# A hybrid decoder layer in split float32: a new order of the first pairs of each FFN, a smaller fold, and the mean added by ScalarE

## The reference

```python
h = rms_norm(x, ffn1_norm[l])
x = x + 0.5 * swiglu(h, ffn1_w1[l], ffn1_w3[l], ffn1_w2[l])   # (silu(h @ w1) * (h @ w3)) @ w2, D_FF = 2816
h = rms_norm(x, mix_norm[l])
proj = h @ w_in[l]                     # q, k, v, z, xBC, dt: attention heads and Mamba-2 heads
...
x = x + concat([attn, ssd]) @ w_out[l]
h = rms_norm(x, ffn2_norm[l])
x = x + 0.5 * swiglu(h, ffn2_w1[l], ffn2_w3[l], ffn2_w2[l])
return rms_norm(x, final_norm)
```

## Time and profile before

| | us |
|---|---|
| median of 3 runs | 582.42 |
| profiled execution, its own time | 582.91 |
| its span | 580.8 |
| TensorE busy | 543.7 (94%) |
| VectorE busy | 438.7 (76%) |
| ScalarE busy | 330.5 (57%) |
| GpSimd busy | 62.2 (11%) |
| bytes moved | 98.15 MB, 169 GB/s in the mean |

### The profile page before, as it was taken

The page is one execution under the profiler, slowest core; times in us unless marked ns, Lnnn a source line. Parts: engine busy times, 40 slices in busy tenths (PEclk is TensorE's granted clock), DMA queues, the critical chain, the costliest instruction groups (busy, mean ns, idle before and its releaser), DMA issues.

```text
span 580.8 us, 9795 instructions
## 1 busy us (share of the span) xinstructions
PE 543.7 (94%) x3676; PEld 500.0 (86%) x3676; DVE 438.7 (76%) x658; ACT 330.5 (57%) x527; POOL 62.2 (11%) x94
## 2 busy tenths in 40 slices
PE   5959999999999989999999999997799999999995
PEld 4948989999999968998888688786699999999993
DVE  3497979888888685768666666558889888888956
ACT  4455556555555466766765874356456555565543
POOL 1000300000000160330532002010000000000014
PEclk9997999999999999999999999999799999999999
DMA  8935776665555438465524225252656665555401
GB/s 249 320 119 181 199 255 217 217 217 172 188 171 186 139 126 247 146 183 157 169 73 146 73 89 179 95 197 62 204 193 217 217 217 178 185 177 183 144 1 72
DMA packets 69434, 98.15 MB, mean 169 GB/s; under 512 B 1812, under 2 KB 55248, under 8 KB 69408
## 3 DMA queue, kind: packets, MB, share of 16 engines
q1 hardware_dynamic: 68560, 95.34, 51.0%
q0 software_dynamic: 848, 2.47, 1.6%
HBM read 96.75 MB, written 1.05 MB: 168 GB/s over the span
## 4 chain that ended last, share of the span: by engine, by line
PE 78%; DVE 8%; DMA 5%; ACT 4%; issue 2%; POOL 1%; SPq 0%; POOLq 0%; DVEq 0%; ACTq 0%
PE bank L1349 24%; PE bank L1350 24%; PE bank L1351 24%; DMA raw<-in_ffn_w 5%; DVE w_lo L915 2%; ACT w_hi L543 2%; PE bank L1481 1%; ACT decay L792 1%; ACT z_silu L571 1%; DVE x_tok L1031 1%; DVE x L929 1%; POOL mean_sq L439 1%; PE bank L1629 1%; PE bank L1630 1%; PE bank L1616 1%
## 5 line engine op out<-in xcount | busy, mean ns | idle before, releaser
L1349 PE MATMUL bank<-hT_hi,w_hi 128*128 128x256 f32 x736 | 210.8, 286 | 13.3 <-DVE tok_rows L1050 13.3
L1350 PE MATMUL bank<-hT_lo,w_hi 128*128 128x256 f32 x736 | 210.1, 285 | 0.0
L1351 PE MATMUL bank<-hT_hi,w_lo 128*128 128x256 f32 x736 | 209.9, 285 | 0.0
L915 DVE TENSOR_TENSOR w_lo<-raw,w_hi 128x1024 fp32r<-128x1024 f32 x132 | 163.5, 1243 | 31.9 <-ACT w_hi L543 31.2
L543 ACT ACTIVATE w_hi<-raw 128x1024 fp32r<-128x1024 f32 x132 | 138.8, 1056 | 61.4 <-PE bank L1351 37.9
L1349 PEld LDWEIGHTS bank<-hT_hi,w_hi 128*128 128x128 f32 x736 | 142.9, 194 | 16.1 <-issue 13.3
L1350 PEld LDWEIGHTS bank<-hT_lo,w_hi 128*128 128x128 f32 x736 | 143.0, 194 | 1.5
L1351 PEld LDWEIGHTS bank<-hT_hi,w_lo 128*128 128x128 f32 x736 | 143.0, 194 | 0.0
L1349 PE MATMUL bank<-w_hi,hT_hi 128*128 128x512 f32 (+1 forms) x192 | 70.1, 365 | 1.4 <-DVE w_lo L915 1.1
L1351 PE MATMUL bank<-w_hi,hT_lo 128*128 128x512 f32 (+1 forms) x192 | 68.2, 355 | 0.0
L1350 PE MATMUL bank<-w_lo,hT_hi 128*128 128x512 f32 (+1 forms) x192 | 68.0, 354 | 0.0
(11 more groups left out here) (198 smaller groups left out, 794.1 us busy)
## 6 DMA issues: line engine op xcount, KB each, us to landing
raw<-in_ffn_w SPq DMA_DIRECT2D x54, 1024.0 KB, 5.4
raw<-in_w_in SPq DMA_DIRECT2D x16, 1024.0 KB, 5.5
tok_rows<-in_ffn_w SPq DMA_DIRECT2D x10, 1024.0 KB, 4.9
raw<-in_w_out SPq DMA_DIRECT2D x6, 1024.0 KB, 4.9
raw<-in_ffn_w SPq DMA_DIRECT2D x4, 512.0 KB, 7.6
x<-in_x SPq DMA_DIRECT2D x4, 256.0 KB, 4.1
out_x<-normed SPq DMA_DIRECT2D x4, 256.0 KB, 2.0
norm_w<-in_ffn_norm SPq DMA_DIRECT2D x1, 512.0 KB, 6.4
```

The lines of the kernel that those rows point to most:

```text
L915: dve.tensor_tensor(lo, src, hi, ALU.subtract).then_inc(half_ready, 1)
L1349: pe.matmul(dst, lhs[0], rhs[0], start=start, stop=False, skip_group_check=True)
L1350: pe.matmul(dst, lhs[0], rhs[1], start=False, stop=False, skip_group_check=True)
L1351: return pe.matmul(dst, lhs[1], rhs[0], start=False, stop=stop, skip_group_check=True)
```

## The change

It has five parts.

1. **First pairs.** `first_pair` of ScalarE and VectorE takes the work on w2 (left half, sums, corner) to its head, and split (1, 1, 0) before the copy of the transposed product. Pair 1 gets a list of its own, `second_pair`, in which the silu stands first.
2. **Slots.** In FFN 1 the odd halves lie in slots 3 and 5 (2 and 3 before) and the rest of w2 in slot 2 (5 before). So mix half 1 no longer waits for the last second products, and mix half 2 does.
3. **Fold.** Two of the four sums are left out; product 5 is added straight to the right quarters of x by VectorE (`fold_right`). GpSimd still adds four times, in the order (0,0), (0,1), (1,1), (1,0); in FFN 1 `row_rstd(1, 0)` stands ahead of the last.
4. **Mean.** GpSimd adds EPS to the left half's sum as soon as that is there; ScalarE adds the right half's sum to it; GpSimd takes the power. This is done in all four norms of 1024 columns.
5. **Rows.** After FFN 1 the second 128 rows are scaled and weighed in one VectorE instruction for each half (`scale_both`), the first 128 not. After FFN 2 the left halves are (`norm_left`). VectorE's and ScalarE's lists after FFN 1 change order: `mix_hi(2)` comes ahead of the squares, the constants and the dt weights go behind. `keep_clock` ahead of z0 writes z0's bank.

```diff
-FFN_SLOT = ((0, 1, 2, 3), (2, 3, 0, 1))
-SPLIT_LEFT, SPLIT_REST = 4, 5
+FFN_SLOT = ((0, 1, 3, 5), (2, 3, 0, 1))
+SPLIT_LEFT, SPLIT_REST = 4, (2, 5)
...
+            def row_rstd(n, t):
+                r = 2 * (n % 2) + t
+                pool.wait_ge(sq_ready, sq_count(n, t) + 1)
+                pool.tensor_scalar(mean_sq[:, r:r + 1], sumsq[:, 0, r:r + 1], EPS, None, ALU.add).then_inc(left_mean_ready, 1)
+                pool.wait_ge(mean_ready, 2 * n + t + 1)
+                pool.tensor_tensor(rstd[:, r:r + 1], row_mean[:, r:r + 1], minus_half[:, :], ALU.pow).then_inc(rstd_ready, 1)
...
-                for j, (t, c, part) in enumerate(((0, 0, T4), (0, 1, T2), (1, 0, T3), (1, 1, T1))):
+                for j, (t, c, part) in enumerate(((0, 0, T4), (0, 1, T1), (1, 1, T3), (1, 0, T3))):
...
+                    if j in (1, 2):
+                        pool.wait_ge(fold_sum, 4 * n + j)
+                    if j == 3 and n == 0:
+                        row_rstd(1, 0)
...
+                if c == 1:
+                    act.wait_ge(sq_ready, sq_count(n, t) + 2)
+                    act.wait_ge(left_mean_ready, 2 * n + t + 1)
+                    act.activation(row_mean[:, r:r + 1], sumsq[:, 1, r:r + 1], ACT.Identity,
+                                   bias=mean_sq[:, r:r + 1]).then_inc(mean_ready, 1)
...
             def first_pair(n):
 
+                left_hi(n, 0, 0)
                 pair_silu(n, 0)
+                sum4_hi(n, 0)
+                corner_hi(n, 0, 0)
                 act.wait_ge(pair_used, n + 1)
                 ffn_hi(n, 1, 0, 0)
+                sums_hi_part(n, 0)
                 pair_silu(n, 1)
                 ffn_hi(n, 1, 0, 1)
-                left_hi(n, 0, 0)
+                ffn_hi(n, 1, 1, 0)
                 act.wait_ge(pair_T, 2 * n + 2)
                 both = bank[:, PAIR_T_BANK, :].rearrange("p (j l) -> p j l", j=2)
                 act.activation(gu_hi[:, :, :], both, ACT.Copy)
                 act.activation(gu, both, ACT.Copy).then_inc(pair_copied, 1)
-                sum4_hi(n, 0)
-                ffn_hi(n, 1, 1, 0)
                 ffn_hi(n, 1, 1, 1)
+
+            def second_pair(n):
+
+                silu(n, 1, 0)
+                asum_hi_part(n, 0)
+                product_hi(n, 1, 0, P)
+                left_hi(n, 1, 1)
+                ffn_hi(n, 2, 0, 0)
+                sum4_hi(n, 1)
+                ffn_hi(n, 2, 0, 1)
+                silu(n, 1, 1)
+                product_hi(n, 1, 1)
+                ffn_hi(n, 2, 1, 0)
+                ffn_hi(n, 2, 1, 1)
...
+            def norm_left(n, t):
+                dve.wait_ge(rstd_ready, rstd_count(n) + t + 1)
+                r, left = 2 * (n % 2) + t, slice(0, 512)
+                dve.scalar_tensor_tensor(normed[:, t, left], x[:, t, left], rstd[:, r:r + 1], norm_w[:, n % 2, left],
+                                         ALU.mult, ALU.mult).then_inc(scaled_left, 1)
...
+            def fold_right(n, t):
+
                 dve.wait_ge(last_products, 3 * n + 2)
-                half_bank(T2, 5, T1).then_inc(fold_sum, 1)
-                dve.wait_ge(last_products, 3 * n + 3)
-                half_bank(T3, 7, T1).then_inc(fold_sum, 1)
-                dve.wait_ge(fold_sum, 4 * n + 3)
-                half_bank(T1, 5, T3).then_inc(fold_sum, 1)
+                dve.wait_ge(folded, 4 * n + t + 2)
+                xs = x[:, t, 512:1024]
+                dve.scalar_tensor_tensor(xs, bank[:, P_BANK[5], :], 0.5, xs, ALU.mult, ALU.add).then_inc(fold_sum, 1)
...
             def first_pair(n):
 
+                pair_sums(n, 0, 0)
+                pair_sum4(n, 0, 0)
                 pair_mul(n, 0)
+                left_lo(n, 0, 0)
+                sum4_lo(n, 0)
+                corner_lo(n, 0, 0)
                 ffn_lo(n, 1, 0, 0)
+                sums_lo_part(n, 0)
                 pair_mul(n, 1)
                 ffn_lo(n, 1, 0, 1)
-                pair_sums(n, 0, 0)
-                pair_sum4(n, 0, 0)
-                left_lo(n, 0, 0)
+                ffn_lo(n, 1, 1, 0)
                 dve.wait_ge(pair_copied, n + 1)
                 dve.tensor_tensor(gu_lo[:, :, :], gu, gu_hi[:, :, :].bitcast(f32), ALU.subtract).then_inc(gu_split, 2)
-                sum4_lo(n, 0)
-                ffn_lo(n, 1, 1, 0)
+                operand_sums(n, 0)
                 ffn_lo(n, 1, 1, 1)
-                operand_sums(n, 0)
+
+            def second_pair(n):
+                up_silu(n, 1, 0)
+                asum_lo_part(n, 0)
+                pair_sums(n, 1, 1)
+                pair_sum4(n, 1, 1)
+                product_lo(n, 1, 0, P)
+                left_lo(n, 1, 1)
+                ffn_lo(n, 2, 0, 0)
+                sum4_lo(n, 1)
+                ffn_lo(n, 2, 0, 1)
+                up_silu(n, 1, 1)
+                operand_sums(n, 1)
+                ffn_lo(n, 2, 1, 0)
+                product_lo(n, 1, 1)
+                ffn_lo(n, 2, 1, 1)
...
+            mix_lo(1)
+            update_x(1, 0, 0)
+            fold_right(0, 0)
+            update_x(1, 0, 1)
+            weigh_x(1, 0, 0)
+            weigh_x(1, 0, 1)
+            scale_left(1, 0)
+            update_x(1, 1, 0)
+            fold_right(0, 1)
+            update_x(1, 1, 1)
+            norm_lo(1, 0)
+            mix_lo(2)
+            scale_both(1, 1)
+            mix_lo(3)
+            norm_lo(1, 1)
...
             ffn_steps(1)
+            fold_right(1, 0)
             update_x(3, 0, 0)
             update_x(3, 0, 1)
-            weigh_x(3, 0, 0)
+            fold_right(1, 1)
+            weigh_x(3, 0, 1)
             update_x(3, 1, 0)
-            weigh_x(3, 0, 1)
             update_x(3, 1, 1)
-            scale_left(3, 0)
-            weigh_x(3, 1, 0)
             weigh_x(3, 1, 1)
-            scale_left(3, 1)
+            norm_left(3, 0)
+            norm_left(3, 1)
```

More of the change, by code:

```diff
@@ L496, in _ @@
             for t in range(TT):
-                rsqrt(2 * t + 2, t, D)
+                row_rstd(0, t)
             pool.wait_ge(first_products, 2)
@@ L503, in _ @@
             pool.dma_start(norm_w[:, 0, :], norms[2].partition_broadcast(P)).then_inc(norm_loaded[2], 16)
-            for t in range(TT):
-                rsqrt(4 + 2 * t + 2, 2 + t, D)
-            pool.wait_ge(weighed, 4)
+            row_rstd(1, 1)
+            pool.wait_ge(scaled_right, 4)
             pool.dma_start(norm_w[:, 1, :], norms[3].partition_broadcast(P)).then_inc(norm_loaded[3], 16)
@@ L523, in _ @@
             rotate(k_tok)
+            for col in range(4, 10):
+                mix_rstd(col, col + 5)
             for t in range(TT):
-                rsqrt(8 + t + 1, 4 + t, 512)
+                row_rstd(2, t)
+            fold(1)
             for t in range(TT):
-                rsqrt(10 + t + 1, 6 + t, 512)
-            for t in range(TT):
-                rsqrt(12 + t + 1, 8 + t, 512)
-            for n in (2, 3):
-                for t in range(TT):
-                    rsqrt(14 + 4 * (n - 2) + 2 * t + 2, 2 * (n % 2) + t, D)
-                if n == 2:
-                    fold(1)
+                row_rstd(3, t)
         @block.scalar
@@ L1028, in fold_sums @@
             def fold_sums(n):
-                def half_bank(dst, product, other):
-                    return dve.scalar_tensor_tensor(w2_sum[:, dst, :], bank[:, P_BANK[product], :], 0.5,
-                                                    w2_sum[:, other, :], ALU.mult, ALU.add)
                 dve.wait_ge(fold_copied, n + 1)
@@ L1118, in _ @@
                 dve.wait_ge(x_loaded[c], 16)
-            scale_first(0)
+            scale_both(0, 0)
             ffn_lo(0, 0, 0, 0)
@@ L1124, in _ @@
             ffn_lo(0, 0, 0, 1)
-            scale_first(1)
+            scale_both(0, 1)
             ffn_lo(0, 0, 1, 0)
@@ L1366, in columns_product, with product @@
                 return last
-            def product(j, start, stop):
+            def product(n, j, start, stop):
                 a = {name: (gu_hi[:, k, tok(t)], gu_lo[:, k, tok(t)])
@@ L1373, in product @@
                 b11, b21, t4, b22 = (tuple(w[:, slot, c * 512:(c + 1) * 512] for w in (w_hi, w_lo))
-                                     for slot in (SPLIT_LEFT, SPLIT_REST) for c in range(2))
+                                     for slot in (SPLIT_LEFT, SPLIT_REST[n]) for c in range(2))
                 t = [(sums_hi[:, k, :], sums_lo[:, k, :]) for k in range(3)]
@@ L1385, in down_first @@
                 pe.wait_ge(gu_split, FT * n + 2 * i + 2)
-                product(1, start, isinstance(i, int) and i == PAIRS - 1)
-                product(2, start, False)
-                product(4, start, False).then_inc(first_products, 1)
+                product(n, 1, start, isinstance(i, int) and i == PAIRS - 1)
+                product(n, 2, start, False)
+                product(n, 4, start, False).then_inc(first_products, 1)
             def down_second(n, i):
@@ L1395, in down_second @@
                 for j in (6, 5, 7):
-                    last = product(j, start, stop)
```

(9 more changed lines are left out.)

120 lines of the change are left out of this document (65 added, 55 removed).

## The result

The changed kernel takes 568.88 us (median of 4 runs, 568.02 to 569.39) beside 582.6 us for the one before (581.98 to 583.92) on the same chip: a ratio of 0.976, 95% interval 0.9738 to 0.9782. The time is 13.7 us less where 18.8 were forecast, and inside the range of 559.3 to 570.0. The profiled execution took 568.54 us with a span of 566.4, against 582.91 and 580.8: 14.4 us less in the span.

What follows compares the result with a forecast made beforehand. TensorE, busy 543.7 of 580.8 us, bounds the kernel; idle time and slow clock can be gained. Terms -19.6 + 2.6 - 0.5 + 0.4 - 0.2 - 0.7 - 0.8 = -18.8 us gave 563.6 us, range 559.3 to 570.

Steps and rivals of the forecast that it cites:

- rival (a): w3 takes 7.4 us, w1 of pair 3 9.65; new gaps cost 10.4 us; 571.4 us; chance 0.17, whole or part.
- the first term: -19.6 us: TensorE's gaps before the first down products and gate (1,1), with slow clock, removed in both FFNs.
- The two gaps and their slow clock: FFN 1: 1.47 + 6.35 us idle, 2.3 us clock; FFN 2: 1.47 + 6.17 us idle, 1.9 us clock.
- the other gap: TensorE's idle 1.47 us before the first down products in each FFN, forecast to be removed.
- The late load: w1 of pair 3, issued at 46.6, leaves about 1.3 us gap before gate (2,1) in each FFN: +2.6 us.
- After this the loop is the old one: Once the openings of the FFNs are past, the loop over later pairs runs as before: 0 us.
- End of FFN 1: +0.4 us (-0.6 to +1.2): transposes of rows 0 start earlier, but GpSimd's fold behind the power delays z0.
- Ahead of FFN 2 and the tail: -0.7 us from TensorE's wait for rows 1 before FFN 2; -0.8 us from the last update, squares and scaling.
- The start and gate (3,1): -0.2 us at FFN 1's rows 1; -0.5 us because the old 0.81 us gap at 80.66 shrinks.
- (b): Each pair's load is issued late in turn, 18 gaps through both FFNs, 23.4 us; 584.4 us; chance 0.03.
- (c): VectorE has slack, no new gap at all, hand-overs at their good ends; 559.3 us; chance 0.12.
- (d): Gaps close, but moving the mean to ScalarE gains nothing: +1.6 us, 565.2 us; chance 0.66 together with the forecast.

Runs made afterwards that it cites:

- Both shift experiments: The changed kernel with row_mean allocated last: 568.64 us; the kernel before with an unused 16-byte tile in row_mean's place: 584.56 us.

## Why the prediction was right, and where it was off

568.88 us lies inside the range of 559.3 to 570.0, but above the forecast's own range of 561.5 to 567, in the part that was given to rival (a). What carried the forecast is the first term; the others err in both directions.

**The two gaps and their slow clock: right in size.** -19.6 us forecast, -20.15 measured in the two stages up to gate (2,0). The details hold too: w1 of pair 2 issued at 31.77 (32.4 forecast), gate (1,1) at 35.87 without a gap (36.5 with the start of the forecast), gate (2,0) at 44.64 (45.0).

**Its cause was given by half.** "So the wait is one of order ... and it also starts late". For the gap ahead of gate (1,1) the order does carry most: with silu and product of (1,0) first and the loads late it fell from 6.35 to 1.26 us, with the loads early and the old list to 3.01. Two things were missing. The order is that of two lists: the prediction named ScalarE's, and ScalarE's alone left 5.99 us, because VectorE's sums of w2 stood ahead of the product as long. And this gap is not the price: with it nearly closed the time stayed, since the product of (1,1) came no sooner. What the lists of the first pair gave alone is two thirds of the openings' gain (4.2 of 6.2 us an FFN), and 1.5 of that is the other gap. The numbers came out right since the layout by instructions contained all of it.

**The late load: the step that failed.** "a new gap of about 1.3 us is left in each FFN: +2.6 us"; measured +3.87 and +3.89. The place, the releaser and the transfer are those forecast: w1 of pair 3 issued at 47.42 (46.6 forecast), landed in 5.44 us (5.6), product of gate and up ended near 54.7 (54.1), bank 3 wanted near 52.7 (52.9). The issue that came 0.8 us later makes most of the difference between 1.3 us and the pause of 1.97 us. The larger part of the miss is the clock. Here 48 matmuls from 54.72 take 7.32 us up to the next down product, against 5.74 for the pair behind it: 1.6 us in each FFN, 3.2 us in all, which the sum set at nothing, though it had priced the clock for the old gaps. The rows gave no sure price: the earlier trace rows only showed pauses three times as long, and behind the pause of 2.36 us in the earlier trace rows the clock stayed at 1.00 (211.09 to 217.69). The term should have been 2.6 to 4 us for the pauses, and up to 3.2 for the clock, with a chance beside it.

**A term that wasn't there: +1.1 us.** "After this the loop is the old one", and "no instruction is added": true of the instructions, not of the addresses. Both shift experiments show it.

**End of FFN 1.** +0.4 forecast, -0.24 measured. Transposes of rows 0 began 0.76 us earlier in their stage (1.1 forecast) and z0 gave 0.5 of it back (1.5 forecast). GpSimd's fold stands behind the power, as forecast, but `update_x(1, 1, 0)`, which began at 203.18, directly followed VectorE's scaling, and the fold had ended at 203.0. `mix_lo(1)` beside the fold took 1.83 us, not 2.2. The Trainium skill, page "SBUF — State Buffer", section "Who interferes with whom", names VectorE's `tensor_scalar` among the instructions that can take the port pair shared with GpSimd and then exclude each other for a whole instruction; the 1.42 us beside the fold and 0.49 without it agree. The prediction used that section for `mix_lo(1)` alone and not for the scaling.

The row for before was also a favourable one. Its stage to z0 is 5.02 us with the clock at 1.00; in the three other profiles of kernels whose FFN 1 ends as in the kernel before, the clock fell to 0.50 behind the same pause (2.36, 2.36 and 2.19 us) and the stage took 5.84, 6.45 and 6.02 us. The changed kernel took 4.78 in both its profiles, with the clock at 1.00 behind 1.59 us. So -0.24 compares with the best of four; beside the other three the gain is 1.1 to 1.7 us.

**Ahead of FFN 2 and the tail.** -0.67 measured for -0.7; -0.54 for -0.8. In the tail GpSimd's first step is off the path (0.22 us, while the right half is squared) and ScalarE's 0.29 us came in, as forecast; the rest is within what one profile tells.

**The start and gate (3,1).** -0.65 for -0.2, but the second batch starts anywhere from 18.75 to 20.14 us in the profiles of these kernels, old and new ones mixed, so one pair of profiles can't show an effect of the change. -1.01 for -0.5: the gap of 0.81 us did go.

**The rivals.** (a), a late load that costs more, is in part what happened, by the clock and not by a slower transfer (5.44 us); its 571.4 us lie 2.5 above the measured time, the forecast 5.3 below. (b) didn't: no gap is repeated in the loop. (c), no new gap, didn't either. (d), the mean for nothing, is refuted by the stages, 1.4 us, though the medians can't tell it.

## What to carry to other kernels

A gap whose releaser stands behind a transfer can have two causes in series, the order of the lists and the issue of the load; lay out both, in every engine's list, and follow the next load after each move, since a pipeline that is faster in front finds its next load late. A pause of about 2 us on TensorE should be priced twice, as idle time and as the low clock that may follow. When an untouched loop changes its pace, look at what was allocated ahead of its operands.
